# Projections of a delta rule overlapped item by item, with gates moved earlier and five waits moved, in a four-layer float32 kernel

## The reference, cut to what matters

```python
h = rmsnorm(x, g)                      # all projections come from h @ w_in
y_attn = grid_attention(rope(norm(q)), rope(norm(k)), v) @ w_o_attn
qkv = silu(depthwise_conv5(cat[qd, kd, vd]))       # the delta rule's inputs
qd, kd = l2norm(qd) * 64 ** -0.5, l2norm(kd)
o = bidir_gated_deltanet(qd, kd, vd, beta, g)      # chunks of 64, a state per head
y_dn = (rmsnorm(o) * silu(z)) @ w_o_dn
x = x + (sigmoid(gate0) * y_attn + sigmoid(gate1) * y_dn) @ w_out
x = x + (silu(conv3(h2 @ w_gate)) * conv3(h2 @ w_val)) @ w_down    # h2 = rmsnorm(x)
```

```python
h = rmsnorm(x, g)
o_a = nsa(q, kv)                       # compressed, selected and window attention
o_b = forgetting_attention(...)        # logits shifted by a cumulated forget gate
o_m = attention(q_m, rmsnorm(mem) @ w_mem_kv)      # mem: 256 tokens
u = sum(sigmoid(merge_i) * ((o_i * silu(s_i)) @ w_branch_i))
x = x + u @ w_out
```

## Time and profile before

| | us |
|---|---|
| median of 3 runs | 3597.94 (3594.01 to 3600.6) |
| the profiled execution: its time | 3594.16 |
| its span in the trace | 3592.0 |
| TensorE busy | 3352.5 |
| VectorE, ScalarE, GpSimd busy | 1886.3, 1553.6, 198.7 |

### The profile page before, as it was taken

The page is one execution under the profiler, slowest core; times in us unless marked ns, Lnnn a source line. Parts: engine busy times, 40 slices in busy tenths (PEclk is TensorE's granted clock), DMA queues, the critical chain, the costliest instruction groups (busy, mean ns, idle before and its releaser), DMA issues. The chain is left out here.

```text
span 3592.0 us, 61513 instructions
## 1 busy us (share of the span) xinstructions
PE 3352.5 (93%) x26780; PEld 2639.4 (73%) x26780; DVE 1886.3 (53%) x2834; ACT 1553.6 (43%) x2612; POOL 198.7 (6%) x188
## 2 busy tenths in 40 slices
PE   7788899999998897999999988999999979999999
PEld 5577787778875586877788866767788757777787
DVE  5555656665566554655755553453434544444443
ACT  6534223433246433333433354546443456473432
POOL 0022320000000130410000000000000000000000
PEclk9999999999999998999999998999999999999999
DMA  4000013233331000123233231202122312111222
GB/s 141 30 14 31 32 32 112 96 95 98 96 107 47 19 26 25 38 72 100 89 94 100 85 112 48 79 28 71 56 91 71 117 33 82 54 56 62 71 74 91
DMA packets 74925, 249.15 MB, mean 69 GB/s; under 512 B 9249, under 2 KB 10913, under 8 KB 73377
## 3 DMA queue, kind: packets, MB, share of 16 engines
q1 hardware_dynamic: 74656, 245.22, 21.0%
HBM read 237.88 MB, written 6.29 MB: 68 GB/s over the span
## 5 line engine op out<-in xcount | busy, mean ns | idle before, releaser
L488 PE MATMUL psum<-s_h,s_w 128*128 128x512 f32 (+1 forms) x6864 | 1672.6, 400 | 21.1 <-DVE s_h L1830 11.8
L488 PEld LDWEIGHTS psum<-s_h,s_w 128*128 128x128 f32 (+1 forms) x6864 | 1293.2, 190 | 329.8 <-issue 44.1
L1830 DVE TENSOR_TENSOR s_w<-s_stage,s_w 128x1024 fp32r<-128x1024 f32 (+2 forms) x468 | 528.3, 1131 | 430.0 <-ACT s_w L1198 427.8
L1198 ACT ACTIVATE s_w<-s_stage 128x1024 fp32r<-128x1024 f32 (+2 forms) x468 | 450.6, 966 | 294.2 <-PE psum L488 269.2
L488 PE MATMUL psum<-s_ffa,s_w 128*128 128x512 f32 x1056 | 249.0, 396 | 3.8 <-DVE s_ffa L1830 3.8
L488 PEld LDWEIGHTS psum<-s_ffa,s_w 128*128 128x128 f32 x1056 | 197.5, 187 | 54.2 <-DVE s_ffa L1830 6.4
L1198 ACT ACTIVATE s_tmp<-psum 128x512 f32<-128x512 f32 (+4 forms) x180 | 102.8, 571 | 283.2 <-PE psum L488 275.3
L488 PE MATMUL psum<-s_oR,s_w 128*128 128x512 f32 (+1 forms) x960 | 215.6, 375 | 4.0 <-ACT s_E L1198 2.1
L1198 ACT ACT_TABLE_LOAD x168 | 215.5, 1283 | 3.7 <-PEq L2752 0.7
L1198 ACT ACTIVATE s_E<-psum,s_nm 128x256 f32<-128x256 f32 (+3 forms) x224 | 114.5, 516 | 195.3 <-DVE s_nm L1912 195.2
L488 PEld LDWEIGHTS psum<-s_oR,s_w 128*128 128x128 f32 x960 | 165.5, 188 | 37.4 <-issue 2.5
(11 more groups left out here) (255 smaller groups left out, 3490.8 us busy)
## 6 DMA issues: line engine op xcount, KB each, us to landing
s_stage<-w SPq DMA_DIRECT2D x192, 512.0 KB, 3.3
s_stage<-wup SPq DMA_DIRECT2D x88, 512.0 KB, 3.3
s_stage<-wo SPq DMA_DIRECT2D x32, 512.0 KB, 3.3
s_stage<-wdn SPq DMA_DIRECT2D x32, 512.0 KB, 3.6
s_stage<-wdn SPq DMA_DIRECT2D x16, 384.0 KB, 3.1
spill<-s_x SPq DMA_DIRECT2D x2, 2048.0 KB, 8.5
s_stage<-woa SPq DMA_DIRECT2D x16, 256.0 KB, 2.7
s_x<-spill SPq DMA_DIRECT2D x2, 2048.0 KB, 7.8
```

What stands on the lines that cost most here:

```text
L488: return self.e.matmul(out, left, right, start=first, stop=last, skip_group_check=True)
L1198: return self.e.activation(out, src, func, **kw)
L1830: return self.e.tensor_tensor(out, a, b, op)
```

## The change

1. `project` is cut into `project_begin` (product, y, convolution) and `project_end` (all the rest), and `overlapped` runs the end of one item in the turns in which the next one begins.
2. All eight gates of branch d and gate 4 of branch a are made by `plug` (nine items, `PLUGGED`). Gates d6 and d7 lie in the rope tile, which is reloaded later for that. The turns at which gates stand in the stages are new, and the fill runs at 1:1. `ORDER_A` changes.
3. At the start, ScalarE and VectorE convert the second and third weight earlier, and SP loads the second one behind x5.
4. In block 2's front, items are begun early, with three more scratch tiles for ScalarE, and the normed h is made in pieces beside the q products; two silu gates come into the front.
5. In `memory`, Ln and Exp go in pairs, with a yield between the two of the norm; the input is loaded into mkT and mv once q3 is multiplied. A yield more stands in `forgetting`.

```diff
-PLUGS = 6
-ORDER_A = (4, 0, 5, 1, 6, 2, 7, 3)
+PLUGS = 7
+ORDER_A = (5, 0, 6, 1, 7, 2, 4, 3)
+PLUGGED = [("d", c) for c in range(8)] + [("a", 4)]
...
-        beside(plugged(abreast(scalars, begun, delayed(project(0, (1,)), 2)), plug, (0, 1)), fill, 1, 1)
-        beside(plugged(units(0), plug, (4, 5, 21, 22, 33)), fill, 5, 6)
-        beside(plugged(self.chain(l, 0), plug, (0,)), fill, 5, 6)
+        beside(abreast(scalars, begun, delayed(project(0, (1,)), 2)), fill, 1, 1)
+        beside(plugged(units(0), plug, (0, 1, 4, 5, 21, 22)), fill, 1, 1)
+        beside(plugged(self.chain(l, 0), plug, (1, 2, 5, 6, 9, 10, 12, 13)), fill, 1, 1)
...
+    def project(self, l, g, js, *inputs):
+
+        items = [(l, "p", g, s3, j) for s3 in range(3) for j in js]
+        return overlapped((self.project_begin(key, *inputs), self.project_end(key)) for key in items)
...
+def overlapped(items):
+
+    rest = iter(())
+    for head, tail in items:
+        for _ in head:
+            next(rest, None)
+            yield
+        yield from rest
+        rest = tail
+    yield from rest
...
+                self.gate = {("d", c): self.early2[:, c, :] if c < 6 else self.rope[:, 7 - c, :] for c in range(8)}
...
-            if c >= (PLUGS if name == "d" else 4):
+            if name == "a" and c > 4:
...
+    def project_begin(self, key, hi, lo, ht):
+        l, _, g, s3, j = key
+        yield from self.lin_steps(key, self.d["w1"][l, 6 + 4 * s3 + 2 * g + j], 8, hi, lo, ht, 4)
+        self.give(key, ("vec_proj", key, "y", 4))
+        yield
+        yield
...
     def layer2(self, l):
...
-        uppers = self.uppers(("two", l), hi, 8)
+        uppers = self.uppers(("two", l), hi, 4)
+        silu = self.silu_gate(l, 0)
+        more = [m.cE[:, :], m.cPT[:, :], m.cR[:, :]]
+        self.borrow(more)
...
+            if 0 < c < 5:
+                self.qk_begin(keys[c - 1], self.at("vec_scaled", keys[c - 1]), C2["qn"])
+                next(uppers, None)
...
-        together(self.forgetting(l), behind(lambda c: self.ahead(keys[c]), rest, 8, LAG))
+        together(self.forgetting(l), behind(first, rest, 10, LAG))
...
+            if 0 < c < 5:
+                self.scaled_in_place(keys[c - 1], ("two", l))
+                next(normal, None)
+                next(normal, None)
...
         for c in range(8):
             self.e.dma_start(m.x[:, c, :], d["xT"][:, c, :]).then_inc(*self.landed(f"dma_x{c}"))
+            if c == 5:
+                self.one_ahead()
...
+                self.w.wait_ge(*self.prod((L, "q", 3)))
+                self.e.dma_start(m.mkT[:, :, :], d["memT"][:, 0:4, :]).then_inc(*self.landed("dma_mem", l, 0))
```

More of the change, by code:

```diff
@@ L817, in scalars @@
         self.give((key, "tot"), ("act_dn", key, "egt"))
[L819 to L848, removed]
@@ L991, in plug @@
     def plug(self, l, hi, lo, ht):
-        for c in range(PLUGS):
-            yield from self.lin_steps((l, "d", "g", c), self.d["w1"][l, 30 + c], 8, hi, lo, ht, 4, ("act_mix", l, "d", c))
+        for name, c in PLUGGED:
+            yield from self.lin_steps((l, name, "g", c), self.d["w1"][l, (30 if name == "d" else 22) + c], 8, hi, lo, ht, 4, ("act_mix", l, name, c))
     def early(self, l, hi, lo, ht):
@@ L1021, in rest @@
         def rest(c):
[L1022 removed]
+            if c < 4 or c in (4, 6):
                 self.qk((L, "q", c) if c < 4 else kv(c), K_BO, K_PB)
[L1024 removed]
+            elif c < 8:
                 self.turned(kv(c))
[L1026 to L1027 removed]
         def silu_gate(s, c0, per=8):
@@ L1032, in silu_gate @@
                 self.give(key, ("vec_sg", L, s, c))
+        silu = silu_gate(0, 10, 4)
+        self.lin((L, "q", 0), wt[l, 0], 8, rhi, rlo, raw, amid=lambda: self.total(tag))
+        together(self.forgetting(l, rhi, rlo, raw), behind(first, rest, 10, LAG))
         def merge_gates():
@@ L1096, in memory @@
         yield
-        for _ in range(4):
+        for _ in range(5):
             yield
@@ new lines, in project_end @@
+    def project_end(self, key):
+        l, _, g, s3, j = key
+        y, s = self.tmp((key, "y")), self.tmp((key, "s"))
+        dst = s if s3 == 2 else self.m.zs[g][:, s3, j, :]
+        self.w.wait_ge(*self.at("act_proj", key, "t"))
+        self.stt(dst, s, 1.0, y, ALU.add, ALU.mult).then_inc(*self.up("vec_proj", key, "silu"))
+        yield
+        if s3 == 2:
+            return
+        yield
+        self.w.wait_ge(*self.at("act_proj", key, "r"))
+        self.stt(dst, dst, 0.0625 if s3 == 0 else 0.5, s, ALU.mult, ALU.mult).then_inc(*self.up("vec_proj", key, "out"))
+        yield
+        yield
@@ L2223, in plug @@
     def plug(self, l):
-        for c in range(PLUGS):
-            self.ahead((l, "d", "g", c), 1)
+        for name, c in PLUGGED:
+            self.ahead((l, name, "g", c), 1)
             yield
@@ L2271, in layer2, with first @@
         keys = [(L, "q", c) for c in range(4)] + [(L, n, b) for b in range(2) for n in "kv"]
+        silu = self.silu_gate(l, 0)
+        def first(c):
+            if c < 8:
+                self.ahead(keys[c])
+            else:
+                next(silu)
+            if 0 < c < 5:
+                self.scaled_in_place(keys[c - 1], ("two", l))
+                next(normal, None)
+                next(normal, None)
         def rest(c):
             if c < 4:
-                self.scaled_in_place(keys[c], ("two", l))
-                for _ in normal:
-                    pass
                 self.qk(keys[c], m.bq[:, c, :], 0.125, True)
-            elif c % 2 == 0:
+            elif c in (4, 6):
                 self.qk(keys[c], m.bk[:, c // 2 - 2, :], 1.0, True)
-        together(self.forgetting(l), behind(lambda c: self.ahead(keys[c]), rest, 8, LAG))
+            if 5 <= c < 7:
+                next(silu)
+        together(self.forgetting(l), behind(first, rest, 10, LAG))
         g24 = m.g24
@@ L2306, in nsa @@
             return self.attention(L, f, out, ready)
-        lanes([nsa(0), nsa(1)], self.memory(l), self.hidden(l), self.compressed(l), self.silu_gate(l, 0), self.merge_gates(l))
+        lanes([nsa(0), nsa(1)], self.memory(l), self.hidden(l), self.compressed(l), silu, self.merge_gates(l))
         self.ahead((L, "fq", 0))
```

288 lines of the change are left out of this document (176 added, 112 removed).

## The result

The changed kernel takes 3491.11 us (median of 4 runs, 3486.96 to 3496.87) against 3598.33 us for the kernel before on the same chip: ratio 0.9705, interval 0.9685 to 0.9725. The forecast was 3525 with a range of 3465 to 3575. So the sign and the range held, and the gain is 107 us where 69 was forecast.

A forecast was written before the change was run, and what follows sets the result against it. The prediction took TensorE, busy 93% of the span, as the bound, with only idle and low-clock time to win. Terms -4 +10 -16.6 -26.9 -30.2 -7 +6 gave -68.7 from 3594.2, so 3525 us, range 3465 to 3575.

The forecast's parts named there:

- start: Kernel start: earlier weight conversion removes TensorE's 4.54 us wait, net -4 us, bounds -6 and +1.
- chain(0): Block 1's chain(0): moved gates and half products cover waits for u and S; losses 21.3 and 21.6 to 8 each, -26.9 us.
- lanes, with the memory: Block 2's lanes: paired Ln and Exp and a yield win 4 and 3 us; uncovered attention turns cost 3 us twice.
- the part that names the change costs here: Stage 0 of block 1: overlapping puts both lists' products in the same turns, costing +5 us a layer, +10 in all.
- the forecast's five stalls: Stage 0's TensorE stalls: 5.2 (weight), 3.3 and 5.3 (turnings), 3 and 1.6 (second list's end); 18.4 us together.
- I leave half: units(0): about half its loss stays at a 1:1 fill, 17.8 to 9.5 and 17.1 to 8.8 us, -16.6 in all.
- it bounds, narrowly: Block 2's front: TensorE at 7 us a turn against ScalarE 6.2, VectorE 4.7; losses fall to 4 us, -30.2 in all.
- +3 twice: Block 2's lanes: with two silu gates in front, attention's last four turns lack cover, 0.8 us each; 3 us, twice.
- Stage 0 costs nothing: Rival, chance 0.22: stage 0's two lists in step are covered as chain(1) is; 3485 us, down to 3465.
- Handover heavy: Rival, chance 0.11: stage 0 costs +26 us a layer; 3567 us.
- stalls move: Rival, chance 0.04: each wait removed comes back at the next bank or weight; 3590 us or so.
- slower: Rival, chance 0.08: an item's handover between engines, now in four turns instead of eight, bounds everywhere; 3645 us if serial.

The follow-up runs named there:

- e7: Changed kernel with the value item's turning one turn later on all three engines and attention starting one turn later; 3490.2 us, 0.9700 of the kernel before.
- e2: Changed kernel with stage 0's second projection list started one turn earlier and the fill stepped once ahead; 3499.5 us, 0.9722 of the kernel before.
- e5: Changed kernel with projection items serial again, fill kept at 1:1; 3528.5 us, 0.9807 of the kernel before.
- e6: Changed kernel, items still overlapped, with the fill back at 6:5 beside units(0) and chain(0); 3502.8 us, 0.9737 of the kernel before.
- e1: Changed kernel with projection items serial again and the fill back at 6:5 beside units(0) and chain(0); 3528.7 us, 0.9807 of the kernel before.
- e9: Kernel before with only the overlapped projection items added (old gates, 6:5 fill, start and block 2); 3551.67 us, 0.9867 of the kernel before.
- e3: Changed kernel with the eight half gates of chain(0) moved into units(0); 3518.1 us, 0.9783 of the kernel before.
- e4: Changed kernel with block 2's old front back on all engines, its two silu gates back in the lanes; 3526.0 us, 0.9804 of the kernel before.
- e8: Changed kernel with TensorE alone taking the sum over the memory's squares one turn later in block 2; 3490.7 us, 0.9702 of the kernel before.
- e11: Changed kernel with two gates moved from units(0) into stage 0, at turns 8, 9, 12 and 13; 3491.2 us, 0.9705 of the kernel before.
- e12: Changed kernel with two gates moved from units(0) into stage 0, at turns 4, 5, 8 and 9; 3492.0 us, 0.9706 of the kernel before.

## Why the prediction was right, and where its sizes were off

**By the forecast's own windows and formula** (idle time plus 0.225 of the low time), in us, layer 0 and layer 1 of a block:

| term | forecast | measured |
|---|---|---|
| start | -4 | -3.6 |
| stage 0 | +5, +5 | 24.2 to 22.4, 23.3 to 24.5: -1.8, +1.2 |
| units(0) | -8.3, -8.3 | 17.8 to 5.2, 17.1 to 4.9: -12.6, -12.2 |
| chain(0) | -13.3, -13.6 | 21.3 to 9.7, 21.6 to 9.9: -11.6, -11.7 |
| fronts | -15.6, -14.6 | 21.2 to 0.9, 20.1 to 0: -20.3, -20.1 |

The forecast's 19.6 and 18.6 for the fronts are of their second halves; 21.2 and 20.1 are of the whole fronts, printed above. The measured column sums to 93 us, where the forecast had 68 for these rows.

The start is read from the first 32x32 turning, at 76.48 us instead of 80.10; in the other runs with the new start it stands at 76.3 to 79.1, so this term is good to a microsecond or two only. Its mechanism held: the wait of 4.54 us is gone, and 2.01 us stand before the column total, where 1.5 were forecast.

The formula leaves out what the clock costs beyond 0.225 (last section). Lengths between the same two matmuls of the two profiled executions leave nothing out: the three stages took 318.3 and 316.9 us before and take 303.9 and 306.0, with three products more in each layer. Counting 5.74 us, a product at full clock, for each product that changed place, the gains are:

| part | forecast gain | measured gain |
|---|---|---|
| start | 4 | 3.6 |
| stage 0, units(0), chain(0), two layers | 33.5 | 59.7 |
| fronts | 30.2 | 46.2 |
| lanes, with the memory | 1 | -4.1 |
| everything else | 0 | 1.3 |

So of the 38 us that were won beyond the forecast the three stages give 26 and the fronts 16, and the lanes take 5 back. By the formula these stages and fronts won 49 and 40 us of their 60 and 46; most of the 17 us between is the clock, which every term of the sum had too cheap.

**Stage 0.** The step "the part that names the change costs here" was mis-sized: +5 us a layer stood there, and in the changed kernel the stage's loss stayed as it was, at 22.4 and 24.5 us, just under the 25 to 35 that the forecast gave as its sign. The same turns do hold both lists' products, but the 5.2 us for a weight that was worked out did not come; e7 shows that such a stall (8.51 us) stands close by, and seems to depend on what attention does in that turn. e2 shows that the common turn is not the cause of what is lost: with the lists pulled apart the stage idled 4 us more. Of the forecast's five stalls, the turnings came true (2.67, 4.35, 2.55, 2.02). The rule of the Trainium skill (ScalarE: Activation LUTs, What ACT_TABLE_LOAD costs) that would have made this term 11 us a layer larger is not borne out: the loss ended below even the sum that went by 1.28 us.

**units(0).** "I leave half" was the weak step. The mechanisms named there were right in part: e5 shows that at 1:1 the 3.74 us wait goes (e6 that it goes with the double turns too, once the items overlap), and e1 that the sum's 2.85 us is the serial item's. But e5 shows too that the ratio wins nothing while the items are serial, and e9 that overlapping wins most with the old ratio and the old gates. What the forecast booked as a cost in stage 0, with gains from ratio and gates elsewhere, is in truth the largest gain: of the 30 us a layer it makes 20 when it comes first and 18 when it comes last. That it comes from the next product standing between an item's product and its sum is what the rows agree with (the sum's wait is in e1 and not in the changed kernel or e9); no run took the halves apart differently.

**chain(0).** Right: 12 matmuls in nearly each turn, clock 0.95, u never waited for over 0.23 us, and by e3 the gates are worth 12 us a layer at this ratio. 8 us of loss were forecast, 9.7 and 9.9 remain, mostly waits for turnings of the fill's items. The S at its beginning still waits 1.82 us, over the 1 us that was said. What was not seen is that the chain seems to suffer from the fill itself (e9 against e3).

**The front.** Right in mechanism, and "it bounds, narrowly" held almost without a remainder: 0.9 and 0 us where 4 was left. e4 prices it at 35 us, with what it costs in the lanes already taken off; 30 less 6 was forecast.

**Memory and lanes.** e4 has the new memory part beside the old front. Its lanes are together 1314.7 us long, against 1320.7 before the change, so the memory part wins 6.0 us where 7 stood. With the new front they are 1324.8 us long, again with 5.74 us for each gate that left them, so the front costs them 10.1 us where "+3 twice" stood. Most of that is for another reason and in another place than was forecast: the first stretch of layer 0 idles 5.2 us in e4 and 9.2 in the changed kernel, from ScalarE's backlog in the second turn and not from the end of attention without cover. These too are lengths of single profiled executions.

**Rivals.** *Stage 0 costs nothing* names nearly the time that was measured (3485), by luck and not for its reason: it had stage 0 covered as chain(1) is, 10 us a layer better than before, and the stage stayed where it was; the difference came in units(0), the fronts and the clock. *Handover heavy*, *stalls move* and *slower* did not happen; but inside the changed kernel stalls do move, as e7, e8 and e11 each show.

## What to carry to other kernels

When every engine runs in one written order, look for the wait that comes because an item's second half has nothing of its own between producer and consumer, and put the next item's product there; in block 1 of this kernel that was worth more than the cover that the gates gave. Two remedies for one loss do not add: price each with and without the other. And where each engine has work waiting, moving one wait by a turn mostly showed the next one (e7, e8), and cover taken from a neighbouring stage only moved the loss there (e11, e12).

## What was not expected of the hardware

The clock was priced too low. The profiled executions of all fourteen kernels (before, changed and the twelve above) have the same 26780 matmuls, so what TensorE's busy time differs by is mostly clock. It goes from 3309.9 us (e7, 94 us at the low level) over 3331.9 (e3, 159 us) to 3352.5 (before, 201 us). Each microsecond at 1.2 GHz cost 38.7 / 96.0 = 0.40 us between before and changed, and 0.36 by a straight line through all fourteen (correlation 0.98). The forecast took 0.225, half of 0.45, on the ground that half of the low time would be idle. By these numbers 0.36 / 0.45, some 80%, was busy. The low stretches themselves say the same: 164.4 of 200.7 us were busy before, 87.7 of 104.7 in the changed kernel, 76 to 92% in the fourteen. 0.45 of the difference is 34.5 of the 38.7 us; what the other 4 are stays open.

In these kernels the low level often comes behind a gap, when TensorE is at work again. This stretch of the changed kernel follows the 2.42 us wait that ended at 347.79, and two in stage 0, from 150.24 and 157.07, follow the waits that ended at 149.61 and 155.92:

```profile
348.21:355.04 6.83, 6.83 (x46) 5.49 (x44) 2.31 (x4) 2.82 (x5) 0.76 (x2) 0.50 0.14 43
```

At 0.36 to 0.40 the 96 us of low time that went away are worth 13 to 17 us more than by 0.225. The one half for throttled time that the Trainium skill charges (TensorE: Matmul & The Clock Gate, HAM oscillation) is nearer to these runs than the forecast's number, and still above them. The forecast's remark that this half would make the low time worth 5% more is wrong: 0.5 in place of 0.45 is 11% more, and in place of the 0.225 that the sum used it is 2.2 times as much.

The clock also makes part of the spread between executions of one kernel. The changed kernel took 3487.0 and 3487.1 us at a granted clock of 0.985, and 3496.9 at 0.981: 2 x 0.004 x 3487 = 28 us more at the low level, 10 us by 0.36. The fourth, 3495.1 at 0.984, is 8 us slower with only 7 us more low time, so the clock is not all of it. The profile read here is one of the two faster executions.
